# End of the expert stage by column quarters, block 0 prepared in the gather loop, low-rank product moved

## The reference, cut to what matters

```
# first block, end
act = gelu(einsum('thkd,td->thk', expert_down[eid], h))       # 8 heads x 16 picks = 128 experts per token
x2  = x + gt2 * einsum('thk,thkd->td', g * act, expert_up[eid])
x   = rmsnorm(x2) * final_g
# second block, begin
h    = rmsnorm(x) * g_pre
proj = h @ w_in        # pool, attention, gated linear attention, its 16 low-rank columns, memory, gates
kv   = (rmsnorm(mem) * g_mem) @ w_mem_kv
```

## Time and profile before

| | |
|---|---|
| median of three timed runs | 4045.8 us (4037.44, 4045.8, 4048.62) |
| the profiled execution: its own time | 4038.54 us |
| its span from first to last instruction | 4036.8 us |
| TensorE busy | 3148.3 us, 78% |
| GpSimd busy | 2482.0 us, 61% |
| VectorE busy | 1811.1 us, 45% |
| ScalarE busy | 1071.0 us, 27% |
| DMA | 1016.9 MB, mean 252 GB/s, 427 GB/s in the gather loop |
| mean granted TensorE clock | 0.867 |

### The profile page before, as it was taken

One profiled execution on the slowest core, in us unless ns is written; L12 is line 12 of the kernel. 1 busy time (PEld: TensorE's weight loads), 2 busy tenths in 40 slices (PEclk: granted clock), 3 DMA queues, 4 the chain that ended last, 5 costly groups with the idle time before them and its releaser, 6 DMA issues. The chain is left out here.

```text
span 4036.8 us, 34477 instructions
## 1 busy us (share of the span) xinstructions
PE 3148.3 (78%) x11487; PEld 2180.6 (54%) x11487; DVE 1811.1 (45%) x2182; ACT 1071.0 (27%) x1630; POOL 2482.0 (61%) x1175
## 2 busy tenths in 40 slices
PE   8899984779997566555555675559999855999997
PEld 1588773558876344222222222227888743887876
DVE  0567645431022677899776666760000044112121
ACT  1211222134432111111112111124333343444433
POOL 0244472038872456677677777838888611888876
PEclk9899987579998788777678887779999986999999
DMA  9677661025543988999999999955555501656543
GB/s 330 205 279 266 246 241 36 0 104 187 187 156 134 374 366 365 427 427 427 424 425 427 426 425 423 427 245 187 193 191 196 174 20 42 206 190 199 197 157 145
DMA packets 309400, 1016.91 MB, mean 252 GB/s; under 512 B 18456, under 2 KB 20340, under 8 KB 241068
## 3 DMA queue, kind: packets, MB, share of 16 engines
q1 hardware_dynamic: 225552, 455.18, 32.3%
q0 software_dynamic: 73776, 537.03, 31.7%
q10 hardware_dynamic: 9964, 23.34, 2.0%
HBM read 1011.26 MB, written 4.23 MB: 252 GB/s over the span
## 5 line engine op out<-in xcount | busy, mean ns | idle before, releaser
L1419 PE MATMUL banks<-up_rows,pick_diagonal 128*128 128x512 f32 x1024 | 686.6, 833 | 492.6 <-DMA up_rows<-peer_up,picked_experts 463.1
L1022 POOL TENSOR_TENSOR merge_weights_lo<-weight_ring,merge_weights_hi 128x1024 fp32r<-128x1024 f32 x336 | 811.0, 2416 | 259.0 <-ACT merge_weights_hi L1015 258.7
L1022 POOL TENSOR_TENSOR in_weights_lo<-weight_ring,in_weights_hi 128x1024 fp32r<-128x1024 f32 x272 | 657.1, 2426 | 294.8 <-ACT in_weights_hi L1015 294.8
L1419 PEld LDWEIGHTS banks<-up_rows,pick_diagonal 128*128 128x128 f32 x1024 | 266.8, 273 | 893.9 <-issue 839.5
L1650 DVE CUSTOM_DVE_ANT_0 down_rows<-down_rows,h_tokens 128x2048 f32<-128x2048 f32 x256 | 584.9, 2291 | 251.1 <-DMA down_rows<-peer_down,picked_experts 243.5
L1364 POOL DMA_INDIRECT up_rows<-peer_up,picked_experts x256 | 484.0, 1891 | 315.2 <-PE banks L1419 165.8
L1358 POOL DMA_INDIRECT down_rows<-peer_down,picked_experts x256 | 470.4, 1838 | 163.4 <-DVE picked_experts L1596 84.9
L1015 ACT ACTIVATE merge_weights_hi<-weight_ring 128x1024 fp32r<-128x1024 f32 x336 | 355.6, 1061 | 539.5 <-PE banks L1046 539.4
L1015 ACT ACTIVATE in_weights_hi<-weight_ring 128x1024 fp32r<-128x1024 f32 x272 | 286.5, 1061 | 643.3 <-PE banks L1046 480.8
L1044 PE MATMUL banks<-in_weights_hi,h_T_hi 128*128 128x512 f32 x1088 | 430.7, 396 | 9.4 <-POOL in_weights_lo L1022 9.4
L1045 PE MATMUL banks<-in_weights_lo,h_T_hi 128*128 128x512 f32 x1088 | 428.6, 394 | 0.0
(11 more groups left out here) (470 smaller groups left out, 4102.9 us busy)
## 6 DMA issues: line engine op xcount, KB each, us to landing
weight_ring<-w_in SPq DMA_DIRECT2D x232, 1024.0 KB, 4.8
cond_ring<-w_ada SPq DMA_DIRECT2D x64, 1024.0 KB, 5.0
weight_ring<-w_ada SPq DMA_DIRECT2D x32, 1024.0 KB, 5.0
weight_ring<-w_out SPq DMA_DIRECT2D x32, 1024.0 KB, 5.0
weight_ring<-peer_query SPq DMA_DIRECT2D x16, 1024.0 KB, 12.3
weight_ring<-w_ret_out SPq DMA_DIRECT2D x8, 1024.0 KB, 5.0
weight_ring<-w_mlstm_out SPq DMA_DIRECT2D x8, 1024.0 KB, 5.1
weight_ring<-w_mem_kv SPq DMA_DIRECT2D x8, 1024.0 KB, 16.0
```

Of the source, the lines that this page charges most:

```text
L1022: pool.tensor_tensor(self.lo[:, at], ring.tile[:, slot, h * self.HALF:(h + 1) * self.HALF], self.hi[:, at], ALU.subtract).then_inc(ring.us ...
L1419: mm = pe.matmul(ps[:, 4 + b], diag[:, G % 2], up[:, p % ROWS, b * CG:(b + 1) * CG], start=(G % PER_TB == 0), stop=(G % PER_TB == PER_TB - ...
```

## The change

- **Ring and rows.** SyncE loads the row g_pre (broadcast to 128 partitions, 1 MB) into mem's place once mem is turned. The first four tiles of w_in wait for dot product 252 of 256. SyncE waits at the end of the phase for the stores of x.
- **Last group.** VectorE's `add_even` is left out for group 127; TensorE adds the even row too, with a third diagonal (ScalarE), and signals after each bank. VectorE multiplies its sum so far by gt2 and adds x at once, then does the same per bank of 512 columns; GpSimd multiplies each quarter by final_g; ScalarE squares by quarters, having loaded the root's table before.
- **Block 0 in the loop.** Its variances and roots are computed at groups 70 to 74. At group XN (104) VectorE scales x by pre_rstd and g_pre; at groups 105 to 109 TensorE turns four blocks of 128 per group, ScalarE copies 512 columns to h_T_hi and VectorE subtracts into h_T_lo.
- **Block 1 behind the stage's end**, by quarters in the same way. The prelude of the second projection goes.
- **Low-rank product.** After the first run of 20 turns TensorE multiplies h_T_hi and h_T_lo with w_lr split into hi and lo: 48 matmuls. ScalarE and GpSimd split w_lr between the runs; VectorE copies the result at the end of the phase.
- h_T_lo is laid out by token block first; three places that read or write it follow.

```diff
-        diag = sb("pick_diagonal", [P, 2, P])
+        diag = sb("pick_diagonal", [P, 3, P])
...
+        g_pre, xn = mem[0], (h2[:, 0], down[:, 0])
+        FILLS_X = KB // 4
+        part = lambda ap, f: ap[:, f * CG:(f + 1) * CG]
...
+        XN = KV + KV_PIECES + 2
...
             for n in range(1, N_KV):
                 load_tiles(sp, ring, turn_of(io["w_mem_kv_2"][0], slice(n * CG, (n + 1) * CG)), base + N + n)
+            sp.wait_ge(mem_turned, KB // 2)
+            sp.dma_start(g_pre, io["g_pre_2"][0].partition_broadcast(P)).then_inc(g_pre_in, 16)
+            sp.wait_ge(dot_done, TB * PICKS - ROWS)
             load_tiles(sp, ring, turn_of(io["w_in_2"][0], slice(0, CG)), base + N + N_KV)
-            sp.wait_ge(xf_ready, TB)
+            sp.wait_ge(xf_ready, 1 + FILLS_X)
             sp.dma_start(e.x_rows[:, 1], e.x[:, 1]).then_inc(e.x_kept, 16)
+            sp.wait_ge(e.x_kept, 16 * TB)
...
+            for f in range(FILLS_X):
+                pool.wait_ge(x2_ready, 1 + f + 1)
+                pool.tensor_tensor(part(e.x[:, 1], f), part(acc[:], f), part(final_g, f), ALU.mult).then_inc(xf_ready, 1)
...
+            def turn_xn(tb, f):
+                fill = tb * FILLS_X + f
+                pe.wait_ge(xn_ready, 1 if tb == 0 else 2 + f)
+                if fill >= 2:
+                    pe.wait_ge(lo_out, fill - 1)
+                for a in range(4):
+                    tr = pe.transpose(ps[:, fill % 2, a * P:(a + 1) * P], xn[tb][:, (4 * f + a) * P:(4 * f + a + 1) * P], e.ident[:])
+                tr.then_inc(xn_turned, 1)
...
             for G in range(GROUPS):
                 p = 2 * G + 1
-                pe.wait_ge(diag_ready, G + 1)
-                pe.wait_ge(up_landed[p % ROWS], in_turn(p))
+                pe.wait_ge(diag_ready, G + 2 if G == GROUPS - 1 else G + 1)
+                q = p - 1 if G == GROUPS - 1 else p
+                pe.wait_ge(up_landed[q % ROWS], in_turn(q))
                 if G == PER_TB:
                     pe.wait_ge(sum_taken, 1)
+                if G == GROUPS - 1:
+                    for b in range(4):
+                        pe.matmul(ps[:, 4 + b], diag[:, 2], up[:, (p - 1) % ROWS, b * CG:(b + 1) * CG], start=False, stop=False, skip_group_check=True)
+                    pe.wait_ge(up_landed[p % ROWS], in_turn(p))
                 for b in range(4):
                     mm = pe.matmul(ps[:, 4 + b], diag[:, G % 2], up[:, p % ROWS, b * CG:(b + 1) * CG],
                                    start=(G % PER_TB == 0), stop=(G % PER_TB == PER_TB - 1), skip_group_check=True)
-                mm.then_inc(odd_added, 1)
+                    if G == GROUPS - 1:
+                        mm.then_inc(bank_summed, 1)
+                if G < GROUPS - 1:
+                    mm.then_inc(odd_added, 1)
...
+                if 0 <= G - (XN + 1) < FILLS_X:
+                    if G == XN + 1:
+                        pe.wait_ge(kv_out, N_KV * TB)
+                    turn_xn(0, G - (XN + 1))
+            for f in range(FILLS_X):
+                turn_xn(1, f)
...
+            def copy_hi(tb, f):
+                fill = tb * FILLS_X + f
+                act.wait_ge(xn_turned, fill + 1)
+                act.activation(e.hT_hi[:, 4 * f:4 * f + 4, tb * P:(tb + 1) * P], ps[:, fill % 2].rearrange("p (a t) -> p a t", a=4),
+                               ACT.Copy).then_inc(hi_out, 1)
...
+                    act.activation(diag[:, 2], e.ident[:], ACT.Copy, scale=share[:, first:first + 1]).then_inc(diag_ready, 1)
...
+                if G == TAIL + 8:
+                    act.wait_ge(x2_var, 1)
+                    act.activation(var[:, :, 0], var[:, :, 0], ACT.Sqrt).then_inc(x2_root, 1)
...
+                if 0 <= G - (XN + 2) < FILLS_X:
+                    copy_hi(0, G - (XN + 2))
+
+            act.activation(unused[:], e.ident[:, 0:1], ACT.Sqrt)
+            for f in range(FILLS_X):
+                act.wait_ge(x2_ready, 1 + f + 1)
+                act.activation(part(down[:, 1], f), part(acc[:], f), ACT.Square, accum_out=parts[:, 0, f:f + 1]).then_inc(x2_squared, 1)
+                if f:
+                    act.wait_ge(xf_ready, 1 + f)
+                    act.activation(part(down[:, 2], f - 1), part(e.x[:, 1], f - 1), ACT.Square, accum_out=parts[:, 1, f - 1:f]).then_inc(xf_squared, 1)
+            act.wait_ge(xf_ready, 1 + FILLS_X)
+            act.activation(part(down[:, 2], FILLS_X - 1), part(e.x[:, 1], FILLS_X - 1), ACT.Square, accum_out=parts[:, 1, FILLS_X - 1:]).then_inc(xf_squared, 1)
+            act.wait_ge(x2_var, 2)
+            act.activation(var[:, :, 1], var[:, :, 1], ACT.Sqrt).then_inc(x2_root, 1)
+            for f in range(FILLS_X):
+                copy_hi(1, f)
...
+            def copy_lo(tb, f):
+                fill = tb * FILLS_X + f
+                dve.wait_ge(hi_out, fill + 1)
+                if f == 0:
+                    dve.wait_ge(e.x_kept, 16 * (tb + 1))
+                dve.tensor_tensor(e.hT_lo[:, tb, 4 * f:4 * f + 4], ps[:, fill % 2].rearrange("p (a t) -> p a t", a=4),
+                                  e.hT_hi[:, 4 * f:4 * f + 4, tb * P:(tb + 1) * P], ALU.subtract).then_inc(lo_out, 1)
...
-                add_even(G)
+                    dve.wait_ge(even_added, PER_TB)
+                    dve.wait_ge(odd_added, PER_TB)
+                    dve.tensor_tensor(acc[:], acc[:], up_sum, ALU.add).then_inc(sum_taken, 1)
+                    dve.wait_ge(tail_in, 32)
+                    dve.wait_ge(sum_taken, 1)
+                    step(dve.tensor_tensor(acc[:], acc[:], gt2, ALU.mult))
+                    dve.tensor_tensor(e.x[:, 0], e.x[:, 0], acc[:], ALU.add).then_inc(x2_ready, 1)
+                if G < GROUPS - 1:
+                    add_even(G)
                 if G == TAIL + 3:
                     dve.wait_ge(x2_squared, 1)
-                    final_gain(0, e.x[:, 0])
+                    dve.tensor_tensor(e.x[:, 0], e.x[:, 0], final_g, ALU.mult).then_inc(xf_ready, 1)
+                if G == TAIL + 6:
+                    dve.wait_ge(xf_squared, 1)
+                    variance_x2(0)
+                    variance_xf(0)
+                if G == TAIL + 10:
+                    inverse_roots(0)
+                if G == XN:
+                    dve.wait_ge(g_pre_in, 16)
+                    dve.scalar_tensor_tensor(xn[0], e.x[:, 0], pre_rstd[:, 0:1], g_pre, ALU.mult, ALU.mult).then_inc(xn_ready, 1)
+                if 0 <= G - (XN + 2) < FILLS_X:
+                    copy_lo(0, G - (XN + 2))
...
-            take_sum(1)
-            residual(1, acc[:])
-            final_gain(1, acc[:])
-            dve.wait_ge(x2_squared, TB)
-            step(dve.tensor_scalar(var[:, 0], sums[:, 0], 1.0 / D, EPS, ALU.mult, ALU.add))
-            step(dve.reciprocal(inverse[:], var[:, 0]))
-            dve.wait_ge(xf_squared, TB)
-            step(dve.scalar_tensor_tensor(var[:, 1], sums[:, 1], 1.0 / D, inverse[:], ALU.mult, ALU.mult))
-            dve.tensor_scalar(var[:, 1], var[:, 1], EPS, None, ALU.add).then_inc(x2_var, 1)
-            dve.wait_ge(x2_root, 1)
-            step(dve.reciprocal(var[:], var[:]))
+            dve.wait_ge(even_added, GROUPS - 1)
+            step(dve.tensor_tensor(acc[:], acc[:], gt2, ALU.mult))
+            step(dve.tensor_tensor(e.x[:, 1], e.x[:, 1], acc[:], ALU.add))
+            for f in range(FILLS_X):
+                dve.wait_ge(bank_summed, f + 1)
+                step(dve.tensor_tensor(part(acc[:], f), ps[:, 4 + f], part(gt2, f), ALU.mult))
+                dve.tensor_tensor(part(acc[:], f), part(e.x[:, 1], f), part(acc[:], f), ALU.add).then_inc(x2_ready, 1)
+            dve.wait_ge(x2_squared, 1 + FILLS_X)
+            step(dve.tensor_reduce(sums[:, 0, 1:2], parts[:, 0], AX, ALU.add))
+            variance_x2(1)
+            dve.wait_ge(xf_squared, 1 + FILLS_X)
+            step(dve.tensor_reduce(sums[:, 1, 1:2], parts[:, 1], AX, ALU.add))
+            variance_xf(1)
+            inverse_roots(1)
+            for f in range(FILLS_X + 1):
+                if f < FILLS_X:
+                    dve.scalar_tensor_tensor(part(xn[1], f), part(e.x[:, 1], f), pre_rstd[:, 1:2], part(g_pre, f), ALU.mult, ALU.mult).then_inc(xn_ready, 1)
+                if f == 1:
+                    dve.wait_ge(xn_ready, 1 + 2)
+                if f:
+                    copy_lo(1, f - 1)
             step(dve.tensor_copy(e.final_rstd[:], var[:, 0]))
...
+                    act.wait_ge(lr_in, 16)
+                    act.activation(w_lr_hi[:], w_lr[:], ACT.Copy).then_inc(lr_hi_ready, 1)
...
+                    pool.wait_ge(lr_hi_ready, 1)
+                    pool.tensor_tensor(w_lr_lo[:], w_lr[:], w_lr_hi[:], ALU.subtract).then_inc(lr_lo_ready, 1)
...
+                    pe.wait_ge(lr_lo_ready, 1)
+                    for k in range(KB):
+                        hi, lo = e.hT_hi[:, k], e.hT_lo[:, :, k]
+                        pe.matmul(ps[0:16, 2, 0:T], w_lr_hi[:, k], hi, start=(k == 0), stop=False)
```

(7 more changed lines are left out.)

106 lines of the change are left out of this document (33 added, 73 removed).

## The result

| | before | changed |
|---|---|---|
| median | 4044.15 us (4 runs) | **4081.78 us** (4074.73 to 4091.44, 4 runs) |
| ratio, 95% interval | | **1.0096** (1.0071 to 1.0122) |
| profiled span | 4036.8 us | 4089.7 us |
| DMA in the gather loop | 427 GB/s | 420 GB/s |
| TensorE busy | 3148.3 us | 3198.7 us |

The account below looks back on a forecast made before the run. Taking the gather loop as DMA-bound, nothing overlapping after it and TensorE full in the second projection, it summed -2.9 - 15.7 + 2.0 + 5.5 + 0.4 = -10.7 us against 4044.2: 4034 us, range 4022 to 4044.

Parts of the forecast that it names:

- term 5: Low-rank product moved into the second projection, where TensorE never idles: +5.5 us, copy of its result +0.4, new layout 0.
- the interval of VectorE's even addition is 9.81 us: Sign of being right: gather-loop groups where w_in was loaded take 9.81 us each.
- 2, block 0: Block 0's normalising and transposes inside the gather loop, covered by the queue of eight rows in flight: 0 us.
- Term 1: Ring loads: w_in out of the gather loop -10.7 us, beside the last gathers +5.3, g_pre row +2.5; sum -2.9.
- The loads win the queue: Rival: all four w_in loads pass before the last gathers, ring loads become +2.5, sum -5.3, 4039 us; chance 17%.
- Term 3: End of the expert stage, last gathered row to second projection's first product: 30.6 us instead of 46.3, -15.7 us.
- Term 4: Second projection's start: TensorE, having idled 7 us, begins at the low clock, +2.0 us (0 to 3.2).
- the lean seam: Rival before the second projection: TensorE warm, no VectorE-GpSimd waits, smaller load share; up to -16.4 us, 4028; chance 25%.

Follow-up runs that it names:

- e2: Changed kernel with 32 unused bytes where pre_rstd was, so later tensors are back at their old addresses: 4026.18 us, ratio 0.9959 to before.
- e1: Changed kernel unaltered, run again on the same chip and in the same rounds as the next three runs: 4080.51 us, ratio 1.0087 to before.
- e13: e6 with the four w_in loads one wait later and 128 bytes ahead of two split-weight sets; all product buffers on multiples of 256: 4017.66 us.
- e16: e14 with 6 unread products behind the last transpose instead of 14: 4014.56 us, ratio 0.9934 to before.
- e7: e2 without the wait that holds back the first four w_in loads: 4035.23 us, ratio 0.9980 to before.
- e8: e2 with the four w_in loads held back until all 256 dot products are done: 4023.95 us, ratio 0.9955 to before.
- e3: Kernel before with final_rstd and pre_rstd in one tensor, so later tensors lie 32 bytes lower: 4095.67 us, ratio 1.0120 to before.
- e4: Kernel before with 64 unused bytes behind pre_rstd, so later tensors lie 64 bytes higher: 4085.17 us, ratio 1.0107 to before.
- e6: Changed kernel with gaps putting ring, h_T and all behind on multiples of 256, except two split-weight sets at 128: 4041.59 us, ratio 0.9994.
- e10: e6 with the four loads one wait later as in e8 and 128 unused bytes ahead of each pair of split weights: 4027.89 us, ratio 0.9961.
- e9: e8 with everything behind final_rstd, except ring and h_T's place in 256, moved by 128 bytes: 4063.76 us, ratio 1.0051 to before.
- e14: e13 with matrix products nobody reads: 14 behind the last transpose, 18 at the second projection's head: 4017.53 us, ratio 0.9933 to before.
- e12: e8 with matrix products nobody reads behind the last up-row sum and the transposes, against TensorE's rest: 4024.39 us, ratio 0.9953 to before.

## Why the prediction was wrong

**The step that failed** is a term that the prediction put at nothing, unsaid: where the tensors lie. Its sum has five terms, all of them operations, waits and bytes, and it takes the loop's 9.81 us a group and the product's pace over from the kernel before. Nearest to the subject is the end of term 5, "The new layout of h_T_lo changes no count and no width: 0". That sentence itself holds (e2 has the new layout and the old rate), but its reasoning, that only counts and widths cost, was applied unsaid to the removal of pre_rstd, which moved the gathers' rows and the weights. Of the signs that it named, "the interval of VectorE's even addition is 9.81 us" is the one that did not come: it was 9.97. Set against e2, which has the same operations in the same order, the changed kernel's trace is 66.5 us longer: 20.1 ahead of the stage, 23.3 in it (19.8 of these are 124 groups by 0.16), 13.8 in the second projection, 9.3 behind. By medians it is 54 to 56; the traces compare the slowest run of the one with the fastest of the other, and the repeated unaltered kernel (e1) began its stage 5.9 us earlier than the first trace. Nothing in the list of operations could show this; a listing of the tensors' places, before and after, would have.

**The rest of the sum** can be read in e2, against the kernel before:

| term | forecast | measured in e2 |
|---|---|---|
| 1, ring loads and g_pre in the loop | -8.2 | -8.3 (first to 125th addition) |
| 1, stretch of the last gathers | +5.3 | +4.0 |
| 2, block 0 | 0 | 0: groups at 9.81 where it is turned |
| 3, end of the last dot product to the first product | -15.7 | -15.9 |
| 4, clock | +2.0 | +2.0 (e13 against e16) |
| 5, low-rank product | +5.5 | +5.7 |
| 5, copy; all else from the first product on | +0.4 | +2.6 |
| ahead of the stage | 0 | -3.7 |
| **sum** | **-10.7** | **-13.6** (spans 4036.8 and 4023.2) |

- *Term 1.* In the last groups of the changed kernel the two queues again share by packets. DMA queues, 2690 to 2715 us, changed kernel (columns as in the earlier trace rows):

```profile
q0 software_dynamic: 1142, 8.30, 80.4%
q1 hardware_dynamic: 1004, 2.01, 21.2%
```

  and SyncE's loads, timeline:

```profile
2691.69 13.56 SPq L168 DMA_DIRECT2D weight_ring<-w_in  x4
```

  The forecast had 8.1 MB in 24.3 us with 2.2 of the loads beside them. "The loads win the queue" did not happen.
- *Term 3.* The product starts 33 us behind the last dot product, but the way there differed, and that 15.9 comes so near to 15.7 is in part luck. TensorE did not begin at the last arrival: it waited for ScalarE's diagonal (2716.66 and 0.39) and began with the even row at 2717.10, 1.5 us behind the dot product, and the last up row landed under these products. Source lines of the tile up_rows in e2, 2655 to 2660 us:

```profile
L1376 POOL DMA_INDIRECT up_rows<-peer_up,picked_experts x1: 2202/2202/2202, 2658.0 to 2658.0; - x1
DMA to landing us min/median/max: 18.1/18.1/18.1
```

  That is a landing at 2676.1, 4.0 us behind the last dot product, where the prediction had 2.7. From this last arrival, which is the prediction's own mark, the product is 29.1 us away in e2, 17.2 less than before, and the last gathers are 5.3 longer; the table has less of both because it cuts at the dot product. What TensorE won by its early start it lost again to the clock: eight matmuls of the even row took 6.57 us, seven of them at the lower clock, some 0.85 apart, where five such ones were forecast. The clock level at this place differs from run to run: from the last dot product to the last h_T_lo it was 27.5 us in e2, 26.2 in e13 and 24.5 in e16, whose sixteen matmuls all ran at the higher level. A quarter took 1.9 us, from 2726.68 to 2728.58, where the prediction had 2.1.
- *Term 4.* Twelve products 0.43 apart instead of 0.23, 2.4 us, of which e16 got 2.0 back.
- *Term 5.* TensorE had no slack. Source lines of the tile w_lr_hi, changed kernel, answering to the earlier trace rows:

```profile
L1867 PE MATMUL banks<-h_T_hi,w_lr_hi x16: 276/280/280, 3198.9 to 3204.2; 128*16 128x256 f32 x16
```

- The other 2.2 us behind the first product and the 3.7 ahead of the stage were not followed up. The start of the stage moved between 1332.0 and 1337.3 us in the traces of e2, e7 and e8, which differ only behind it, so 3.7 is inside the spread.

So the time in e2, 4026.2 us, lies in the range, 8 us below the point, and the lean seam's 4028 is nearer than the forecast, though for other reasons than it gave. Of the table's terms none was off by more than 2.2 us, apart from the start of the stage; the term that was missing was worth some 55.

**Not settled.** Which accesses of a product collide was not tried apart: the stationary h_T and the moving weights both lie in the same memory, and only their distance was varied. That half a multiple (128) and 224 cost the same 3%, and 64 only 1%, is unexplained, and so is that 128 costs the first merges less. When the expert stage begins depends on addresses too: 1346 to 1352 us in the changed kernel, e3 and e4 against 1332 to 1337 in the kernel before and in e2, e7, e8, 1323 to 1332 in e6, e13 to e16, and 1345.9 in e10, whose first merges and first projection have h_T and weights 128 apart. It comes in part from the loads of w_ada into cond_ring, for which VectorE waited longer, in part from the products' rate, and was not divided further; unaltered kernels differ by some 6 us in it. Waits of the tile cond_ring (us, times), changed kernel, then before:

```profile
  DMA cond_ring<-w_ada: 105.7, 37
```

```profile
  DMA cond_ring<-w_ada: 82.6, 31
```

## What to carry to other kernels

When an edit adds or drops a tensor, however small, list the places of the large buffers before and after: put the targets of large gathers on multiples of 256 bytes, and the two operands of a product at the same remainder by 256. If a stretch that an edit does not touch changes its pace at full busy share, look there first, and try the unchanged kernel with the same shift. And judge a change only once both kernels have good addresses: here the same edit was worth +38 us, or -19 with 32 unused bytes (e2).

## What the runs showed of the hardware

- A gather of 128 rows of 8 KB at 427 GB/s takes 1.3% longer with its target 64 or 128 bytes off a multiple of 256, and 1.6% at 224 off (9.81, 9.94, 9.97 us for four).
- TensorE's products of 128x512, fp32 in two rounded parts, busy throughout at the granted clock of 1.00 (2.4 GHz), stand 0.227 us apart in the second projection with h_T and weights 0 apart by 256 (e2, e10, e13), 0.229 at 64 (e4), 0.232 to 0.233 at 128 (e9, e6) and 0.233 at 224 (changed kernel); in the first merges 0.227 at 0 (e9, e13) and 0.230 to 0.232 at 128 (before, e10). The row of busy time shows full use in all of them; only the count tells.
- The Trainium skill ("SBUF — State Buffer", SBUF: two separate sides) has TensorE waiting for nobody at SBUF. These runs do not show whether or on whom it waits, only that with other operand places it does 3% less. The same page's section on operand start alignment asks for a multiple of the element size, which every address here kept.
- Unread products brought TensorE's clock to the higher level of 2.4 GHz, and it was still there after 1.2 us of rest (e14, e16); after a rest of 5.3 us (e12) it was at 1.2 GHz for the next 12 products.
